# Chunkwise mLSTM: the work of a chunk split into three parts that run one and two chunks apart

## The chip, the cores and the metric

One core of a Trainium2 chip. The metric is the device time of one execution in microseconds (us), the median of several runs. TensorE is called PE, VectorE DVE, ScalarE ACT, GpSimd POOL and SyncE SP in the rows.

## What is computed

Three transformer blocks run one after the other on one sequence of 1024 tokens with 1024 features. The change is in the first block, in its mLSTM branch, which has 4 heads of 128 features and walks the sequence in 8 chunks of 128 tokens:

```python
def step(carry, inp):
    C, n, m = carry
    qb, kb, vb, ib, bb = inp
    d = bb[..., :, None] - bb[..., None, :] + ib[..., None, :]
    d = jnp.where(tri, d, -jnp.inf)
    g = bb + m[..., None]
    m_t = jnp.maximum(g, jnp.max(d, axis=-1))
    s_qk = jnp.einsum('bhtk,bhsk->bhts', qb, kb) * jnp.exp(d - m_t[..., None])
    inter = jnp.exp(g - m_t)
    num = (jnp.einsum('bhts,bhsv->bhtv', s_qk, vb)
           + inter[..., None] * jnp.einsum('bhvk,bhtk->bhtv', C, qb))
    den = jnp.sum(s_qk, axis=-1) + inter * jnp.einsum('bhk,bhtk->bht', n, qb)
    h = num / jnp.maximum(jnp.abs(den), jnp.exp(-m_t))[..., None]
    ...
    C_new = decay[..., None, None] * C + jnp.einsum('bhs,bhsv,bhsk->bhvk', wa, vb, kb)
    n_new = decay[..., None] * n + jnp.einsum('bhs,bhsk->bhk', wa, kb)
    return (C_new, n_new, m_new), h
```

Everything that depends on the running maximum m is known for all tokens before the chunks begin (rows R1, R4 and the columns COL in the kernel). Only C and n pass from chunk to chunk.

## The kernel before

The kernel is written by hand: each engine has one function for each block (`pe_block1`, `dve_block1`, `act_block1`), its instructions run in the order in which they are written, and the engines are tied by semaphores. The large products of all three blocks take their weights from one stream of 131 slots, which SP loads, POOL splits into a high and a low part, and PE uses in order. PE's products of one slot take about 22 us in block 1. Two slots of split weights and two of raw ones are held ahead of PE.

The mLSTM chunks use no streamed weights. For each of the 8 chunks the kernel before runs, in this order of dependence:

- PE, line 724: the row R4 spread over 128 partitions (bank 0), 4 products; the row R1 likewise (bank 1), line 727; then `bc_ready`. Then the keys transposed (bank 3, line 731, `kt_ready`) and the scores of keys and queries (bank 2, line 735, `sc_ready`). Each product of two fp32 operands shows as two instructions in the trace, a transpose as one.
- DVE, line 1076: the exponents into the tile EW (4 instructions, one for each head), `e_done`; ACT, line 908: the exponential over EW, `w_exp`. DVE meanwhile, lines 1079 to 1085: the scaled queries QS, the decay DEC, the weighted keys KW. Then line 1090: EW times the scores, the weights between tokens, `pt_done`.
- PE, lines 714 and 716: the numerators, from EW and the values and, from the second chunk on, QS and the state CS (banks 4 and 5), `num_ready`; line 719: the update of the state from KW (banks 6 and 7), `cu_ready`.
- DVE, lines 1095 to 1120: the new state CS, `c_done`; four small instructions for the denominator; the output h into QT (line 1112), `h_done`; its statistics (bn_stats and bn_aggr).
- ACT, line 910, sends for the sigmoid of the next chunk's output gate (OSC, two buffers) after each exponential. Line 1112 needs it.

There is one buffer each of EW, QS, KW and of every bank, and DVE's chunk begins with the exponents of this chunk, after the statistics of the last. The loop of PE is written with the second half of chunk c - 1 ahead of the first half of chunk c:

```python
for c in range(NT + 1):
    if c >= 1:
        pe.wait_ge(S("pt_done"), c)
        wait(pe, S("c_done"), c - 1)
        ...                                  # numerators and update of chunk c - 1
    if c < NT:
        ...                                  # rows, transposes, scores of chunk c
```

After the eighth chunk PE goes on with the queries of the differential attention (`q_d`, line 438), two slots that have been split long before.

Of the kernel before, what the change touches and what calls it, by code (L numbers as in the profile page):

```python
# [23 lines left out]
ACT = mybir.ActivationFunctionType  # L24
AX = mybir.AxisListType.X

P = 128
# [114 lines left out]
class Line:  # L142
# [10 lines left out]
    def wait(self, n=None):  # L153
        self.eng.wait_ge(self.sem, self.n if n is None else n)
# [16 lines left out]
def build(nc, xT, memT, stream, params, wqkv, sgu, bias2, lru_w, metaT, outT, o_scr, h_scr, blocks=(1, 2, 3)):  # L171
    TL, WH = plan(blocks)
    NSLOT = len(TL) // TILES
    with ExitStack() as ctx:
# [10 lines left out]
                 "ff_raw": ("d_sq", 32), "weight_step": ("lam_v", 2), "meta_step": ("lam_a", 1), "final_step": ("d_sd", 1), "f_sq": ("mv_done", 8),  # L185
# [19 lines left out]
        def at(name, offset, shape, dt=F32):  # L205
            return nc.alloc_sbuf_tensor_at(name, shape, dt, offset=base + offset)
# [363 lines left out]
        if 1 in blocks:  # L570
# [18 lines left out]
            EW = at("e_w", CH, [P, H1, P])  # L589
# [70 lines left out]
        def pe_block1(pe):  # L660
# [47 lines left out]
            for c in range(NT + 1):  # L708
                if c >= 1:

                    pe.wait_ge(S("pt_done"), c)
                    wait(pe, S("c_done"), c - 1)
                    for h in range(H1):
                        mm = nc.tensor.matmul(num(h), EW[:, h, :], V1[:, c - 1, h, :], start=True, stop=(c == 1))
                        if c > 1:
                            mm = nc.tensor.matmul(num(h), QS[:, h, :], CS[:, h, :], start=False, stop=True)
                    mm.then_inc(S("num_ready"), 1)
                    for h in range(H1):
                        mm = nc.tensor.matmul(cup(h), KW[:, h, :], V1[:, c - 1, h, :], start=True, stop=True)
                    mm.then_inc(S("cu_ready"), 1)  # L720
                if c < NT:
                    for h in range(H1):
                        sel = IDENT[0:4, h:h + 1].to_broadcast([4, P])
                        nc.tensor.matmul(ps[:, P * h:P * (h + 1)], sel, R4[:, P * c:P * (c + 1)], start=True, stop=True)
                    for h in range(H1):
                        sel = IDENT[0:4, h:h + 1].to_broadcast([4, P])
                        mm = nc.tensor.matmul(ps[:, BANK + P * h:BANK + P * (h + 1)], sel, R1[:, P * c:P * (c + 1)],
                                              start=True, stop=True)
                    mm.then_inc(S("bc_ready"), 1)
                    for h in range(H1):  # L730
                        mm = nc.tensor.transpose(ps[:, 3 * BANK + P * h:3 * BANK + P * (h + 1)], KT[:, h, P * c:P * (c + 1)],
                                                 IDENT)
                    mm.then_inc(S("kt_ready"), 1)
                    for h in range(H1):
                        mm = nc.tensor.matmul(ps[:, 2 * BANK + P * h:2 * BANK + P * (h + 1)], KT[:, h, P * c:P * (c + 1)],
                                              QT[:, h, P * c:P * (c + 1)], start=True, stop=True)
                    mm.then_inc(S("sc_ready"), 1)

            slot, quad = WH["q_d"]
# [102 lines left out]
        def act_block1(act):  # L844
# [60 lines left out]
            act.dma_start(OSC[:, 0, :], o_scr[0]).then_inc(S("o_back0"), 16)  # L905
            for c in range(NT):
                act.wait_ge(S("e_done"), c + 1)
                nc.scalar.activation(EW[:, :, :], EW[:, :, :], ACT.Exp).then_inc(S("w_exp"), 1)
                if c + 1 < NT:
                    act.dma_start(OSC[:, (c + 1) % 2, :], o_scr[c + 1]).then_inc(S(f"o_back{(c + 1) % 2}"), 16)  # L910
            act.wait_ge(S("mv_done"), NT)
            nc.scalar.activation(SD[:, :], MV[:, :, 1], ACT.Sqrt, bias=EPSC).then_inc(S("sd_done"), 1)

# [103 lines left out]
        def dve_block1(dve):  # L1017
# [54 lines left out]
            for c in range(NT):  # L1072
                dve.wait_ge(S("bc_ready"), c + 1)
                wait(dve, S("num_ready"), c)
                for h in range(H1):
                    ins = nc_v.scalar_tensor_tensor(EW[:, h, :], ps[:, BANK + P * h:BANK + P * (h + 1)], COL[:, c, h:h + 1],
                                                    par("mask_ts", 0, P), ALU.add, ALU.add)
                ins.then_inc(S("e_done"), 1)
                v.step(nc_v.tensor_tensor(QS[:, :, :], ps[:, 0:BANK].rearrange("p (h t) -> p h t", h=H1),
                                          QT[:, :, P * c:P * (c + 1)], ALU.mult))  # L1080
                v.step(nc_v.tensor_copy(DEC[:, :], ps[:, P - 1:BANK:P]))
                dve.wait_ge(S("kt_ready"), c + 1)
                wait(dve, S("cu_ready"), c)
                for h in range(H1):
                    v.step(nc_v.tensor_scalar(KW[:, h, :], ps[:, 3 * BANK + P * h:3 * BANK + P * (h + 1)],
                                              COL[:, c, 4 + h:5 + h], SC1, ALU.mult, ALU.mult))
                dve.wait_ge(S("w_exp"), c + 1)
                dve.wait_ge(S("sc_ready"), c + 1)
                v.wait()
                nc_v.scalar_tensor_tensor(EW[:, :, :].rearrange("p h t -> p (h t)"), ps[:, 2 * BANK:3 * BANK], SC1,  # L1090
                                          EW[:, :, :].rearrange("p h t -> p (h t)"), ALU.mult, ALU.mult).then_inc(S("pt_done"), 1)
                dve.wait_ge(S("cu_ready"), c + 1)
                for h in range(H1):
                    if c == 0:
                        ins = nc_v.tensor_copy(CS[:, h, :], cup(h))
                    else:
                        ins = nc_v.scalar_tensor_tensor(CS[:, h, :], CS[:, h, :], DEC[:, h:h + 1], cup(h), ALU.mult, ALU.add)
                    ins.then_inc(S("c_upd"), 1) if h < H1 - 1 else ins.then_inc(S("c_done"), 1)
                dn = ps[:, 4 * BANK:6 * BANK].rearrange("p (b x) -> p b x", b=2)[:, :, 0:2 * (P + 1)]\
                    .rearrange("p b (h w) -> p b h w", w=P + 1)[:, :, :, P]  # L1100
                v.step(nc_v.tensor_scalar(DN[:, :].rearrange("p (b h) -> p b h", b=2), dn, -1.0, None, ALU.mult))
                v.wait()
                v.step(nc_v.tensor_tensor(DN[:, :].rearrange("p (b h) -> p b h", b=2), dn,
                                          DN[:, :].rearrange("p (b h) -> p b h", b=2), ALU.max))
# [1492 lines left out]
```

## Time and profile before

| | |
|---|---|
| median of 3 runs | 3708.5 us (3707.46 to 3709.02) |
| the profiled execution's own time | 3712.65 us |
| its span | 3710.9 us |
| busy share: PE, DVE, ACT, POOL | 91%, 36%, 20%, 32% |
| mean granted clock of TensorE | 0.956 of full speed |

The span runs from the first to the last instruction of the profiled execution. The chunks lie between about 224 and 328 us of it. A granted clock of 1.00 is TensorE at 2.4 GHz, 0.50 at 1.2 GHz, and a value between is a stretch with some of both. A row "x8" is eight instructions in a run, with the time from the first's start to the last's end.

### The profile page before, as it was taken

To read this page: it belongs to the slowest core of one execution; us is meant where nothing else is said; L and a number is where in the kernel's file an instruction comes from. 1 tells how busy PE (TensorE), PEld (TensorE's weight loads), DVE (VectorE), ACT (ScalarE), POOL (GpSimd) and SP (SyncE) were. 2 spreads that over 40 slices of the span, in tenths; PEclk is the share of its full clock that TensorE was granted. 3 is DMA by queue.
4 is the path that set the end of the run, shared out by engine and by line. 5 is a ranking of instruction groups with operands and counts; after the bars stand their busy time and mean duration, and the time that the engine had idled before them with its cause. 6 is when DMAs were issued, how large, how long until landed. Compare 5 with 4: busy or idle time off the path is not lost.

```text
span 3710.9 us, 37478 instructions
## 1 busy us (share of the span) xinstructions
PE 3375.2 (91%) x15576; PEld 2708.9 (73%) x15576; DVE 1341.0 (36%) x1651; ACT 744.9 (20%) x1082; POOL 1194.3 (32%) x1012
## 2 busy tenths in 40 slices
PE   5967976889959999999999999997997989999997
PEld 4646854778848568877888888886984678888886
DVE  4145055033140450223342111126999662222223
ACT  2220045121021450111211000003442410001011
POOL 3201300525423013324444334433232243443341
PEclk9977998899979899999999999999999999999998
DMA  3100100101221001112111111111202011111111
GB/s 117 47 15 20 53 5 12 68 23 64 84 85 46 23 13 46 66 37 92 46 46 46 57 45 45 46 56 42 80 35 80 23 36 56 45 45 57 45 45 46
DMA packets 31693, 179.62 MB, mean 48 GB/s; under 512 B 3793, under 2 KB 4817, under 8 KB 14673
## 3 DMA queue, kind: packets, MB, share of 16 engines
q1 hardware_dynamic: 18864, 137.37, 10.5%
q10 hardware_dynamic: 12704, 40.42, 2.9%
q8 instruction: 99, 1.62, 0.2%
q14 instruction: 26, 0.20, 0.0%
HBM read 163.10 MB, written 14.68 MB: 48 GB/s over the span
## 4 chain that ended last, share of the span: by engine, by line
PE 82%; DVE 12%; ACT 3%; issue 2%; POOL 1%; DMA 0%; DVEq 0%; ACTq 0%; POOLq 0%
PE ps L438 47%; PE ps L469 16%; PE ps L495 5%; PE ps L1902 3%; DVE c_out L2353 2%; PE ps L1434 1%; PE ps L770 1%; PE ps L1450 1%; ACT p L937 1%; PE ps L678 1%; PE ps L318 1%; PE ps L326 1%; PE ps L1953 1%; DVE soft L1164 1%; DVE p L1639 1%
## 5 line engine op out<-in xcount | busy, mean ns | idle before, releaser
L535 POOL TENSOR_TENSOR whi<-raw,par 128x512 fp32r<-128x512 f32 x121 | 134.3, 1110 | 2150.8 <-PE ps L438 1703.5
L438 PE MATMUL ps<-xhi,whi 128*128 128x512 f32 x2304 | 721.4, 395 | 45.3 <-DVE xlo L379 15.2
L539 POOL TENSOR_TENSOR wlo<-raw,whi 128x512 fp32r<-128x512 f32 x484 | 716.3, 1480 | 38.5
L438 PE MATMUL ps<-xlo,whi 128*128 128x512 f32 x2304 | 716.1, 392 | 0.0
L438 PE MATMUL ps<-xhi,wlo 128*128 128x512 f32 x2304 | 714.9, 392 | 0.0
L438 PEld LDWEIGHTS ps<-xhi,whi 128*128 128x128 f32 x2304 | 434.2, 190 | 148.0 <-issue 24.3
L438 PEld LDWEIGHTS ps<-xlo,whi 128*128 128x128 f32 x2304 | 437.0, 190 | 92.3
L438 PEld LDWEIGHTS ps<-xhi,wlo 128*128 128x128 f32 x2304 | 436.1, 189 | 92.2
L537 POOL CAST whi<-raw 128x512 fp32r<-128x512 f32 x363 | 280.4, 772 | 0.0
L469 PE MATMUL ps<-hidden_hi,whi 128*128 128x512 f32 x864 | 268.6, 392 | 0.4 <-DVE hidden_lo L1314 0.4
L469 PE MATMUL ps<-hidden_lo,whi 128*128 128x512 f32 x864 | 268.8, 392 | 0.0
L469 PE MATMUL ps<-hidden_hi,wlo 128*128 128x512 f32 x864 | 267.1, 390 | 0.0
L1324 DVE TENSOR_TENSOR h<-h,ps 128x1024 f32<-128x1024 f32 x112 | 132.3, 1217 | 350.5 <-PE ps L469 350.5
L1276 ACT ACTIVATE ff_act<-ps 128x1024 f32<-128x1024 f32 x46 | 47.3, 1028 | 976.9 <-PE ps L438 976.9
L469 PEld LDWEIGHTS ps<-hidden_hi,wlo 128*128 128x128 f32 x864 | 162.2, 188 | 36.6
L469 PEld LDWEIGHTS ps<-hidden_lo,whi 128*128 128x128 f32 x864 | 162.3, 188 | 35.8
L469 PEld LDWEIGHTS ps<-hidden_hi,whi 128*128 128x128 f32 x864 | 161.3, 188 | 36.4 <-issue 1.7
L2353 DVE SCALAR_TENSOR_TENSOR c_out<-c_in,par,c_out 128x1024 f32<-128x1024 f32 x120 | 179.1, 1494 | 4.9 <-ACT c_out L2105 1.4
L547 POOL TENSOR_TENSOR wlo<-raw,whi 128x512 fp32r<-128x512 f32 x40 | 83.1, 2107 | 263.4 <-ACT whi L258 263.4
L1305 DVE TENSOR_TENSOR ff_tmp<-ff_act,ps 128x1024 f32<-128x1024 f32 x18 | 22.0, 1221 | 328.0 <-ACT ff_act L1276 328.0
L1310 DVE TENSOR_TENSOR ff_tmp<-ff_act 128x1024 f32<-128x1024 f32 x32 | 41.1, 1285 | 216.2 <-ACT ff_act L1276 216.1
L1314 DVE TENSOR_TENSOR hidden_lo<-ff_tmp,hidden_hi 128x1024 fp32r<-128x1024 f32 x54 | 86.9, 1609 | 63.8 <-ACT hidden_hi L1279 63.8
(458 smaller groups left out, 4149.8 us busy)
## 6 DMA issues: line engine op xcount, KB each, us to landing
raw<-stream SPq DMA_DIRECT2D x131, 1024.0 KB, 4.7
x_in<-xT ACTq DMA_DIRECT2D x4, 1024.0 KB, 14.6
x_again<-xT ACTq DMA_DIRECT2D x4, 1024.0 KB, 8.1
h_scr<-h ACTq DMA_DIRECT2D x1, 4096.0 KB, 12.6
h<-h_scr ACTq DMA_DIRECT2D x1, 4096.0 KB, 13.2
h_scr<-h ACTq DMA_DIRECT2D x4, 1024.0 KB, 4.7
outT<-h ACTq DMA_DIRECT2D x8, 512.0 KB, 3.0
bias<-bias ACTq DMA_DIRECT2D x1, 2560.0 KB, 18.7
```

Of the source, the lines that this page charges most:

```text
L438: mm = nc.tensor.matmul(ps[:, c0 + c:c0 + c + width], w, x(k, a, width), start=(n == 0 and m == 0), stop=(n == len(ks) - 1 and m == 2))
L469: mm = nc.tensor.matmul(ps[:, c0 + c:c0 + c + HALF], w, x(k, a, HALF), start=(k == 0 and m == 0), stop=(k == n - 1 and m == 2))
L495: mm = nc.tensor.matmul(ps[:, c:c + BANK], x(k, P * tt, P), w, start=(k == 0 and m == 0), stop=(k == KB - 1 and m == 2))
L535: nc.gpsimd.tensor_tensor(WHI[:, r, t], RAW[:, r, t], one, ALU.mult).then_inc(hi_done, 1)
L537: nc.gpsimd.tensor_copy(WHI[:, r, t], RAW[:, r, t]).then_inc(hi_done, 1)
L539: ins = nc.gpsimd.tensor_tensor(WLO[:, r, t], RAW[:, r, t], WHI[:, r, t].bitcast(F32), ALU.subtract)
L547: ins = nc.gpsimd.tensor_tensor(WLO[:, r, t], RAW[:, r, t], WHI[:, r, t].bitcast(F32), ALU.subtract)
L1276: nc.scalar.activation(FA[:, j % 2, :], half(q, 0), ACT.Silu if k == "f2" else ACT.Relu)\
L1314: nc.vector.tensor_tensor(HL[:, j, :], FT[:, j % 2, :], HH[:, j, :].bitcast(F32), ALU.subtract)\
L1324: nc.vector.tensor_tensor(stream_tile[:, b, :], stream_tile[:, b, :], half(q, b % 2), ALU.add).then_inc(free(q), 1)
L1902: mm = nc.tensor.matmul(ps[:, c0 + BANK * i:c0 + BANK * i + width], w, x(k, a, width), start=(k == 0 and m == 0), stop=(k == KB - 1 and m ...
L2353: nc.vector.scalar_tensor_tensor(CCO[:, b, :], CC[:, b, META + k:META + k + T], par("cc_conv_w_3", 4 * k + b), CCO[:, b, :], ALU.mult, ALU ...
```

## The change

The same instructions are issued, in another order. PE's work of a chunk is split into `chunk_scores` (the spread of R1 and the scores) and `chunk_rows` (the spread of R4 and the transposes), DVE's into `chunk_exponents`, `chunk_weights`, `chunk_queries` and `chunk_keys`. The scores, exponents and weights of chunk c + 2 are made in the loop's pass c, the scaled queries and weighted keys of chunk c + 1 likewise. EW has two buffers, the second over weights that are no longer needed. QS, KW and the banks stay single. The waits on DVE's own counter for QS, DEC and KW are gone, and PE waits on two new counts, `qs_done` and `kw_done`. ACT sends for the sigmoid of chunk c once h of chunk c - 2 is made, one pass earlier than before.

```diff
+            def chunk_scores(c):
+                wait(pe, S("e_done"), c)
+                for h in range(H1):
+                    ...
+                mm.then_inc(S("bc_ready"), 1)
+                wait(pe, S("pt_done"), c)
+                for h in range(H1):
+                    ...
+                mm.then_inc(S("sc_ready"), 1)
+
+            def chunk_rows(c):
+                if c > 0:
+                    pe.wait_ge(*L("qs_done", 2 * c))
+                for h in range(H1):
+                    ...
+                if c > 0:
+                    pe.wait_ge(*L("kw_done", c))
+                for h in range(H1):
+                    ...
+                mm.then_inc(S("kt_ready"), 1)
+
+            chunk_scores(0)
+            chunk_rows(0)
+            chunk_scores(1)
+            for c in range(NT):
+                pe.wait_ge(S("pt_done"), c + 1)
+                pe.wait_ge(*L("qs_done", 2 * c + 1))
+                wait(pe, S("c_done"), c)
+                wait(pe, S("h_done"), c)
+                for h in range(H1):
+                    ...
+                mm.then_inc(S("num_ready"), 1)
+                pe.wait_ge(*L("kw_done", c + 1))
+                for h in range(H1):
+                    ...
+                mm.then_inc(S("cu_ready"), 1)
+                if c + 1 < NT:
+                    chunk_rows(c + 1)
+                if c + 2 < NT:
+                    chunk_scores(c + 2)
...
-                if c + 1 < NT:
-                    act.dma_start(OSC[:, (c + 1) % 2, :], o_scr[c + 1]).then_inc(S(f"o_back{(c + 1) % 2}"), 16)
+                if c >= 1:
+                    wait(act, S("h_done"), c - 1)
+                    act.dma_start(OSC[:, c % 2, :], o_scr[c]).then_inc(S(f"o_back{c % 2}"), 16)
...
+            chunk_exponents(0)
+            chunk_queries(0)
+            chunk_keys(0)
+            chunk_weights(0)
+            chunk_exponents(1)
+            chunk_weights(1)
+            for c in range(NT):
                 dve.wait_ge(S("cu_ready"), c + 1)
+                dve.wait_ge(*L("qs_done", 2 * c + 2))
...
                 ins.then_inc(S("h_done"), 1)
+                if c + 1 < NT:
+                    chunk_queries(c + 1)
+                    chunk_keys(c + 1)
+                if c + 2 < NT:
+                    chunk_exponents(c + 2)
                 dve.wait_ge(S("h_done"), c + 1)
...
                 ins.then_inc(S("mv_done"), 1)
+                if c + 2 < NT:
+                    chunk_weights(c + 2)
```

On DVE, from the output h of one chunk (q_t) to the next update of the state. Before:

```order
L1112 SCALAR_TENSOR_TENSOR q_t<-ps,denom,o_sig 128x128 x4
L1117 BN_STATS stats<-q_t 128x6 x4
L1120 BN_AGGR mean_var<-stats 128x2 x4
L1076 SCALAR_TENSOR_TENSOR e_w<-ps,cols,par 128x128 x4
L1079 TENSOR_TENSOR q_s<-ps,q_t 128x512
L1081 COPY decay<-ps 128x4
L1085 TENSOR_SCALAR k_w<-ps,cols 128x128 x4
L1090 SCALAR_TENSOR_TENSOR e_w<-ps,e_w 128x512
L1097 SCALAR_TENSOR_TENSOR c_state<-c_state,decay,ps 128x129 x4
```

and of the change:

```order
L1149 SCALAR_TENSOR_TENSOR q_t<-ps,denom,o_sig 128x128 x4
L1109 TENSOR_TENSOR q_s<-ps,q_t 128x512
L1111 COPY decay<-ps 128x4
L1116 TENSOR_SCALAR k_w<-ps,cols 128x128 x4
L1096 SCALAR_TENSOR_TENSOR e_w_379<-ps,cols,par 128x128 x4
L1159 BN_STATS stats<-q_t 128x6 x4
L1162 BN_AGGR mean_var<-stats 128x2 x4
L1104 SCALAR_TENSOR_TENSOR e_w_379<-ps,e_w_379 128x512
L1134 SCALAR_TENSOR_TENSOR c_state<-c_state,decay,ps 128x129 x4
```

The scaled queries, the decay and the weighted keys (of the next chunk) now follow h directly; the exponents and the weights (e_w, first and last row of that tile) belong to the chunk after the next, and the statistics stand between them.

On PE, from the update of the state to the next chunk's numerators. Before:

```order
L719 MATMUL ps<-v_one,k_w 128x129 x4
L724 MATMUL ps<-row_374,par 128x128 x4
L727 MATMUL ps<-row_373,par 128x128 x4
L731 MATMUL ps<-par,k_t 128x128 x4
L735 MATMUL ps<-q_t,k_t 128x128 x4
L714 MATMUL ps<-v_one,e_w 128x129
L716 MATMUL ps<-c_state,q_s 128x129
```

and of the change:

```order
L751 MATMUL ps<-v_one,k_w 128x129 x4
L729 MATMUL ps<-row_374,par 128x128 x4
L733 MATMUL ps<-par,k_t 128x128 x4
L715 MATMUL ps<-row_373,par 128x128 x4
L720 MATMUL ps<-q_t,k_t 128x128 x4
L745 MATMUL ps<-v_one,e_w_379 128x129
L747 MATMUL ps<-c_state,q_s 128x129
```

PE's order within a chunk is nearly the same. What moved is whose they are: the spread of R1 and the scores (L715 and L720) are those of the chunk after the one whose numerators follow.

## Rows read from the trace of the kernel before

**Rows 1.** The chain of waits, 224 to 334 us: start us, us, engine, tile, line.

```profile
236.16 0.89 DVE c_state L1095 x4
...
328.33 5.77 PE ps L438 x24
```

**Rows 2.** Who waited for whom, 228 to 333 us: us in total, times, longest.

```profile
POOL whi L535 <- PE ps L438: 201.9, 1, 201.9
...
DVE c_state L1097 <- PE ps L719: 37.7, 7, 5.6
...
PE ps L714 <- DVE e_w L1090: 31.5, 8, 4.5
```

**Rows 3.** Timeline, last chunk: start us, us, engine line op [idle before <-releaser].

```profile
314.92 1.12 DVE L1097 SCALAR_TENSOR_TENSOR c_state<-c_state,decay,ps 128x129 f32<-128x129 f32 x4 [5.62 <-PE ps L719]
...
316.75 1.13 DVE L1112 SCALAR_TENSOR_TENSOR q_t<-ps,denom,o_sig 128x128 f32<-128x128 f32 x4
...
317.92 0.87 DVE L1117 BATCH_NORM_STATS2 stats<-q_t 128x6 f32<-128x128 f32 x4
...
319.12 1.09 DVE L1076 SCALAR_TENSOR_TENSOR e_w<-ps,cols,par 128x128 f32<-128x128 f32 x4
...
320.13 0.68 DVE L1079 TENSOR_TENSOR q_s<-ps,q_t 128x512 f32<-128x512 f32 x1
...
320.25 0.63 ACT L908 ACTIVATE e_w<-e_w 128x512 f32<-128x512 f32 x1 [12.82 <-DVE e_w L1076]
...
320.80 1.11 DVE L1085 TENSOR_SCALAR k_w<-ps,cols 128x128 f32<-128x128 f32 x4
...
322.05 0.69 DVE L1090 SCALAR_TENSOR_TENSOR e_w<-ps,e_w 128x512 f32<-128x512 f32 x1
...
322.80 0.80 PE L714 MATMUL ps<-v_one,e_w 128*128 128x129 f32 x2 [4.27 <-DVE e_w L1090]
...
326.40 1.93 PE L719 MATMUL ps<-v_one,k_w 128*128 128x129 f32 x8
...
328.37 1.12 DVE L1097 SCALAR_TENSOR_TENSOR c_state<-c_state,decay,ps 128x129 f32<-128x129 f32 x4 [5.62 <-PE ps L719]
```

**Rows 4.** Timeline, second chunk, TensorE after its clock rose.

```profile
247.19 1.06 PE L719 MATMUL ps<-v_one,k_w 128*128 128x129 f32 x8
...
248.18 1.15 PE L724 MATMUL ps<-row,par 4*128 4x128 f32 x8
...
250.65 1.06 PE L735 MATMUL ps<-q_t,k_t 128*128 128x128 f32 x8
```

**Rows 5.** Timeline, first chunk, TensorE.

```profile
224.72 2.04 PE L724 MATMUL ps<-row,par 4*128 4x128 f32 x8 [0.44 <-DVE cols L1068]
...
226.55 1.91 PE L727 MATMUL ps<-row,par 4*128 4x128 f32 x8
...
228.39 1.11 PE L731 MATMUL ps<-par,k_t 128*128 128x128 f32 x4
...
229.30 1.91 PE L735 MATMUL ps<-q_t,k_t 128*128 128x128 f32 x8
...
232.31 2.09 PE L714 MATMUL ps<-v_one,e_w 128*128 128x129 f32 x8 [1.10 <-DVE e_w L1090]
```

**Rows 6.** TensorE by stretches: us, busy (instructions), granted clock, DMA share, GB/s.

```profile
243.80:246.80 3.00, 3.00 (x14) 0.50 0.00 0
246.80:252.00 5.20, 4.91 (x40) 0.99 0.00 0
490.00:610.00 120.00, 88.32 (x587) 0.99 0.00 1
750.00:790.00 40.00, 30.89 (x218) 1.00 0.00 1
350.00:370.00 20.00, 13.92 (x57) 0.74 0.00 1
```

**Rows 7.** The sigmoid tile that comes back from memory, issue to landing.

```profile
DMA to landing us min/median/max: 2.4/2.6/2.7
```

More of the change, by code:

```diff
@@ L184, in build @@
                  "m_sq": ("bc_ready", 8), "m_sum": ("kt_ready", 8), "pads_set": ("sc_ready", 8), "l_cols": ("vt_ready", 8),
-                 "ff_raw": ("d_sq", 32), "weight_step": ("lam_v", 2), "meta_step": ("lam_a", 1), "final_step": ("d_sd", 1), "f_sq": ("mv_done", 8),
+                 "ff_raw": ("d_sq", 32), "qs_done": ("gate_sum", 12), "kw_done": ("qkv_kept", 12), "weight_step": ("lam_v", 2), "meta_step": ("lam_a", 1), "final_step": ("d_sd", 1), "f_sq": ("mv_done", 8),
                  "f_add": ("h_done", 8), "f_x": ("ones_set", 1), "sp_a": ("o_stored", 32), "sp_b": ("rows_a", 6),
@@ L588, in build @@
             CH = XM_AT + 8192
-            EW = at("e_w", CH, [P, H1, P])
+            EW = [at("e_w0", CH, [P, H1, P]), at("e_w1", XM_AT + 20512, [P, H1, P])]
             QS = at("q_s", CH + 2048, [P, H1, P])
@@ L707, in pe_block1 @@
             pe.wait_ge(S("cols_kept"), 1)
[L708 to L737, printed above, removed]
@@ new lines, in chunk_scores @@
+            def chunk_scores(c):
+                wait(pe, S("e_done"), c)
+                for h in range(H1):
+                    sel = IDENT[0:4, h:h + 1].to_broadcast([4, P])
+                    mm = nc.tensor.matmul(ps[:, BANK + P * h:BANK + P * (h + 1)], sel, R1[:, P * c:P * (c + 1)],
+                                          start=True, stop=True)
+                mm.then_inc(S("bc_ready"), 1)
+                wait(pe, S("pt_done"), c)
+                for h in range(H1):
+                    mm = nc.tensor.matmul(ps[:, 2 * BANK + P * h:2 * BANK + P * (h + 1)], KT[:, h, P * c:P * (c + 1)],
+                                          QT[:, h, P * c:P * (c + 1)], start=True, stop=True)
+                mm.then_inc(S("sc_ready"), 1)
@@ new lines, in chunk_rows @@
+            def chunk_rows(c):
+                if c > 0:
+                    pe.wait_ge(*L("qs_done", 2 * c))
+                for h in range(H1):
+                    sel = IDENT[0:4, h:h + 1].to_broadcast([4, P])
+                    nc.tensor.matmul(ps[:, P * h:P * (h + 1)], sel, R4[:, P * c:P * (c + 1)], start=True, stop=True)
+                if c > 0:
+                    pe.wait_ge(*L("kw_done", c))
+                for h in range(H1):
+                    mm = nc.tensor.transpose(ps[:, 3 * BANK + P * h:3 * BANK + P * (h + 1)], KT[:, h, P * c:P * (c + 1)], IDENT)
+                mm.then_inc(S("kt_ready"), 1)
@@ new lines, in pe_block1 @@
+            chunk_scores(0)
[7 more added lines that the diff above has]
+                for h in range(H1):
+                    mm = nc.tensor.matmul(num(h), EW[c % 2][:, h, :], V1[:, c, h, :], start=True, stop=(c == 0))
+                    if c > 0:
+                        mm = nc.tensor.matmul(num(h), QS[:, h, :], CS[:, h, :], start=False, stop=True)
+                mm.then_inc(S("num_ready"), 1)
+                pe.wait_ge(*L("kw_done", c + 1))
+                for h in range(H1):
+                    mm = nc.tensor.matmul(cup(h), KW[:, h, :], V1[:, c, h, :], start=True, stop=True)
+                mm.then_inc(S("cu_ready"), 1)
[3 more added lines that the diff above has]
+                    chunk_scores(c + 2)
@@ L907, in act_block1 @@
                 act.wait_ge(S("e_done"), c + 1)
-                nc.scalar.activation(EW[:, :, :], EW[:, :, :], ACT.Exp).then_inc(S("w_exp"), 1)
-                if c + 1 < NT:
-                    act.dma_start(OSC[:, (c + 1) % 2, :], o_scr[c + 1]).then_inc(S(f"o_back{(c + 1) % 2}"), 16)
+                nc.scalar.activation(EW[c % 2][:, :, :], EW[c % 2][:, :, :], ACT.Exp).then_inc(S("w_exp"), 1)
+                if c >= 1:
+                    wait(act, S("h_done"), c - 1)
+                    act.dma_start(OSC[:, c % 2, :], o_scr[c]).then_inc(S(f"o_back{c % 2}"), 16)
             act.wait_ge(S("mv_done"), NT)
@@ L1071, in dve_block1, with chunk_exponents @@
             dve.wait_ge(S("skip_done"), 4)
-            for c in range(NT):
+            def chunk_exponents(c):
                 dve.wait_ge(S("bc_ready"), c + 1)
-                wait(dve, S("num_ready"), c)
+                wait(dve, S("num_ready"), c - 1)
                 for h in range(H1):
-                    ins = nc_v.scalar_tensor_tensor(EW[:, h, :], ps[:, BANK + P * h:BANK + P * (h + 1)], COL[:, c, h:h + 1],
+                    ins = nc_v.scalar_tensor_tensor(EW[c % 2][:, h, :], ps[:, BANK + P * h:BANK + P * (h + 1)], COL[:, c, h:h + 1],
@@ L1077, in dve_block1, with chunk_weights @@
                                                     par("mask_ts", 0, P), ALU.add, ALU.add)
                 ins.then_inc(S("e_done"), 1)
-                v.step(nc_v.tensor_tensor(QS[:, :, :], ps[:, 0:BANK].rearrange("p (h t) -> p h t", h=H1),
-                                          QT[:, :, P * c:P * (c + 1)], ALU.mult))
-                v.step(nc_v.tensor_copy(DEC[:, :], ps[:, P - 1:BANK:P]))
-                dve.wait_ge(S("kt_ready"), c + 1)
+            def chunk_weights(c):
+                dve.wait_ge(S("w_exp"), c + 1)
+                dve.wait_ge(S("sc_ready"), c + 1)
+                e = EW[c % 2][:, :, :].rearrange("p h t -> p (h t)")
+                nc_v.scalar_tensor_tensor(e, ps[:, 2 * BANK:3 * BANK], SC1, e, ALU.mult, ALU.mult).then_inc(S("pt_done"), 1)
@@ L1083, in dve_block1, with chunk_queries, chunk_keys @@
+            def chunk_queries(c):
+                dve.wait_ge(S("kt_ready"), c + 1)
+                wait(dve, S("num_ready"), c)
+                nc_v.tensor_tensor(QS[:, :, :], ps[:, 0:BANK].rearrange("p (h t) -> p h t", h=H1),
+                                   QT[:, :, P * c:P * (c + 1)], ALU.mult).then_inc(*qs_step)
+                nc_v.tensor_copy(DEC[:, :], ps[:, P - 1:BANK:P]).then_inc(*qs_step)
+            def chunk_keys(c):
                 wait(dve, S("cu_ready"), c)
                 for h in range(H1):
-                    v.step(nc_v.tensor_scalar(KW[:, h, :], ps[:, 3 * BANK + P * h:3 * BANK + P * (h + 1)],
-                                              COL[:, c, 4 + h:5 + h], SC1, ALU.mult, ALU.mult))
@@ L1087, in dve_block1 @@
[L1087 to L1091, printed above, removed]
+                    ins = nc_v.tensor_scalar(KW[:, h, :], ps[:, 3 * BANK + P * h:3 * BANK + P * (h + 1)],
+                                             COL[:, c, 4 + h:5 + h], SC1, ALU.mult, ALU.mult)
@@ L1092, in dve_block1 @@
+                ins.then_inc(S("kw_done"), 1)
+            qs_step = (S("qs_done"), 1)
+            chunk_exponents(0)
[5 more added lines that the diff above has]
+            for c in range(NT):
                 dve.wait_ge(S("cu_ready"), c + 1)
+                dve.wait_ge(*L("qs_done", 2 * c + 2))
                 for h in range(H1):
```

## Prediction

> **What bounds the kernel now.** I read the chain of waits first, to see whether the chunks lie on the path that sets the end. They do: it runs from the first state update at 236.16 to the products of `q_d` at 328.33 without a piece of other work [rows 1]. The eighth update starts at 328.37 [rows 3], so the seven chunk periods take (328.37 - 236.16)/7 = 13.17 us each. The table of who waited for whom says how such a period is made up: DVE waits for PE's line 719 for 37.7 us in 7 times and PE waits for DVE's line 1090 for 31.5 us in 8 times [rows 2]. Neither engine is full. They take turns.
>
> The timeline of the last chunk gives the turns [rows 3]. DVE works from the update at 314.92 to the end of the weights at 322.05 + 0.69 = 322.74, 7.82 us. PE then makes numerators and update, and DVE starts again 328.37 - 322.80 = 5.57 us later. 7.82 + 0.06 + 5.57 = 13.45. PE's other work (rows, transposes, scores) lies beside DVE's turn already and costs nothing today.
>
> The clock is part of it. Of the 5.57 us, 16 products take 326.40 - 322.80 = 3.60, or 0.22 us each [rows 3]. In the second chunk the granted clock is 0.50 in the first 3 us and 0.99 in the next 5.2 [rows 6], and there 8 products take 248.18 - 247.19 = 0.99, or 0.12 each [rows 4]. The idle turn drops TensorE to 1.2 GHz, and the numerators, the only part on the path, pay for it. At 2.4 GHz they and the update would be 24 x 0.124 + 0.1 = 3.1 us. Rows, transposes and scores are 250.65 + 1.06 - 248.18 = 3.53 at 2.4 GHz.
>
> **The change, step by step.** *What stays between updates.* No arithmetic is added or removed. The exponents, ACT's exponential and the weights of a chunk are now made nearly two passes before their numerators. What PE still waits for behind an update is the state, the denominator, h, and the scaled queries. The DVE pieces by [rows 3], start to start: update and denominator 316.75 - 314.92 = 1.83; h 1.01 (taken from 320.13 - 319.12, four instructions with no wait behind them; with the wait for h in front of the statistics it is 1.17); queries 0.68; signal 0.06. PE starts 3.58 us after the update starts. The next update can start 3.58 + 3.1 = 6.7 us after the last if TensorE runs at 2.4 GHz, and 3.58 + 5.57 = 9.15 at 1.2 GHz.
>
> *What DVE needs in all.* It issues the same instructions, 7.82 us by rows. Two waits on its own results fall away: behind h (1.17 - 1.01 = 0.16) and between the keys and the weights (322.05 - 320.80 = 1.25 against 1.01, so 0.24). That leaves 7.42; for the four waits on semaphores that are new in a pass I add 0.1, my estimate: **7.5 us**. The Trainium skill (VectorE: DVE Perf Modes, "The DRAIN you can't avoid") says that a semaphore between two DVE operations costs nothing extra. These rows disagree, for a wait on the operation just before. By the page the period would be 7.8, and the time 2 us more.
>
> *What PE needs in all.* 3.1 + 3.5 = 6.6 us at 2.4 GHz, beside DVE's 7.5. So DVE sets the pace, PE is 88% busy, and the 3.5 us of rows and scores lie in the 3.58 us in which PE waits for the queries; at 1.2 GHz they would not. Of PE's queue: `q_d` stands behind the last update only; the scores of chunk c + 2 wait for the weights of chunk c + 1, which DVE ended before it began this pass.
>
> *ACT and the transfer.* The exponential, 0.63 us [rows 3], has the statistics on DVE as cover, 319.12 - 317.92 = 1.20 us; without them DVE would wait 0.7. ACT's new wait for h stands in front of its DMA; that h was made before the exponents that ACT has just handled, so nothing queued behind it (the next exponential) is late. The sigmoid lands 2.6 us after issue [rows 7] and is wanted more than one pass later. SP and POOL get no new wait. POOL has stood 201.9 us waiting for PE when `q_d` begins [rows 2], so the weights are split and `q_d` simply starts earlier.
>
> *The start.* More must be done before the first numerators. Before, the first update starts 236.16. Now PE makes at 1.2 GHz the spread of R1, the scores and the spread of R4 (8 instructions each, 226.55 - 224.72 = 1.83) and 4 transposes (229.30 - 228.39 = 0.91) [rows 5]: ready at 224.72 + 6.4 + 0.2 = 231.3. DVE adds queries and decay 0.67, keys 1.01, weights 0.7: 233.8. Scores of chunk 1, 1.84, then numerators and update as before (236.16 - 232.31 = 3.85 [rows 1, 5]): 239.5 if the clock stays low. It rose near 236 before; I take 239.0, so **+2.8 us**.
>
> *The sum.* Pass 0: 7.3 (its update is a copy, 0.15 shorter). Passes 1 to 5: 5 x 7.5 = 37.5. Pass 6 makes no exponents or weights, so DVE needs 5.9 and the path through PE, 6.7, decides. 239.0 + 7.3 + 37.5 + 6.7 = 290.5, and 0.5 more because pass 0 may begin at the low clock: 291.0. Before: 328.37. **Saved: 37.4 us.** Behind the loop nothing changes but the start. The profiled execution has a span of 3710.9 and its own time is 3712.65; the sum makes that 3675.3. It lies 4.15 above the median of the runs, 3708.5, and the same step off the median gives **3671 us**.
>
> *The clock.* This is the term that the trace before does not show: TensorE 88% busy with gaps near 1 us. Nearest rows: in the memory attention it is busy 30.89 of 40 us with clock 1.00, and in the differential attention 88.32 of 120 at 0.99, both with small products and short gaps [rows 6]. Against them stand the transposes from 350 us on, busy 13.92 of 20 us at 0.74. The new loop is busier than all three, so I take 1.00, and keep 1.2 GHz throughout as the other end. Part of its work are products over 4 rows only; in [rows 5] the clock stays low through them.
>
> The Trainium skill (TensorE: Matmul & The Clock Gate, "A second HAM failure mode: psum-queue depth-cycling") warns that frequent short idles between groups of matmuls make the clock go up and down. By it the answer would be rival B; the two attention rows of this case do not bear it out, the transposes do.
>
> **The rivals.** *A, the forecast:* high clock, DVE sets the pace. 3671, chance 0.75.
>
> *B, the clock swings.* It is low when the numerators start, high for the rows and scores. Period 9.15: 239.5 + 7 x 9.15 = 303.6, saved 24.8: **3684**. For it: the transposes in [rows 6]. Chance 0.15.
>
> *C, low clock all through.* PE needs 24 products 5.3 + 6.4 = 11.75 a chunk and sets the pace itself: 239.5 + 6 x 11.75 + 9.15 = 319.2, saved 9.2: **3699**. [...] Chance 0.04.
>
> *D, slower: the scores in lockstep.* There is one bank of scores, and PE's scores stand ahead of the numerators in its queue. If their wait were ended only by the last DVE instruction of the same pass, at the low clock, a period would be DVE's 7.42, scores 1.91, numerators and update 5.57, 14.9: 239.5 + 6 x 14.9 + 9.15 = 338, 9.7 later: **3718**. It is slower than before from a period of 13.3 us. Against it: the count in that wait asks for the weights of one pass earlier. Chance 0.03.
>
> *E, the gain does not arrive.* The chunks shrink, but a later stage that runs on a schedule of its own (split weights, loads) holds `q_d` or its successors: **3708**. Against it: POOL's 201.9 us. Chance 0.03.
>
> **How the numbers follow.** The prediction is A's 3671. Its own bounds: the start with the high clock throughout (1.5 less), a DVE period of 7.2 (1.8 less), 2 to 3 us of run differences: 3665. Upward B's 3684 and 2 us for a slower warm-up: 3686. That holds A and B, nearly 0.9; C, D and E are left out. A change below 0.2% (7.4 us) can't be told from none: A, B and most of C lie beyond it, faster 0.93; same 0.04 (E and the rest of C); slower 0.03.
>
> **What would show it.** In the trace after: the updates (c_state) some 7.5 us apart in passes 1 to 5, first near 239, last near 291; DVE with no idle time to speak of before them; PE's wait for the scaled queries near 1 us; numerators at 0.12 us an instruction and a granted clock near 1.00 from 245 to 290. Updates 9 us apart with numerators at 0.22 us would be B, 12 us apart with PE never idle C, PE idle ahead of the scores D, idle PE ahead of line 438 E. The sum is wrong if DVE's instructions grow longer beside a busy PE, or if the first update comes after 241.

## The result and the profile after

| | before | after |
|---|---|---|
| median of 4 runs | 3708.76 us | 3676.84 us (3669.43 to 3679.06) |
| span of the profiled execution | 3710.9 us | 3675.2 us |
| its granted clock | 0.956 | 0.959 |

The ratio is 0.991, interval 0.9892 to 0.9927: 31.9 us faster. For the runs made later, the kernel before had medians of 3712.3 to 3712.9, and each is compared with the one of its own group. All runs were in the same fast state but one execution of the kernel before in the last group (6841.41 us), which the ratios leave out.

Timeline of the kernel after, VectorE's state updates, and the first products of `q_d`:

```profile
239.94 0.89 DVE L1132 COPY c_state<-ps 128x129 f32<-128x129 f32 x4 [2.67 <-PE ps L751]
...
248.29 1.12 DVE L1134 SCALAR_TENSOR_TENSOR c_state<-c_state,decay,ps 128x129 f32<-128x129 f32 x4 [1.12 <-PE ps L751]
...
255.66 1.11 DVE L1134 SCALAR_TENSOR_TENSOR c_state<-c_state,decay,ps 128x129 f32<-128x129 f32 x4
263.04 1.12 DVE L1134 SCALAR_TENSOR_TENSOR c_state<-c_state,decay,ps 128x129 f32<-128x129 f32 x4
...
270.41 1.11 DVE L1134 SCALAR_TENSOR_TENSOR c_state<-c_state,decay,ps 128x129 f32<-128x129 f32 x4
...
278.66 1.13 DVE L1134 SCALAR_TENSOR_TENSOR c_state<-c_state,decay,ps 128x129 f32<-128x129 f32 x4 [0.79 <-PE ps L751]
...
286.78 1.12 DVE L1134 SCALAR_TENSOR_TENSOR c_state<-c_state,decay,ps 128x129 f32<-128x129 f32 x4 [0.65 <-PE ps L751]
...
294.67 0.79 PE L438 MATMUL ps<-xhi,whi 128*128 128x512 f32 x2
295.03 1.13 DVE L1134 SCALAR_TENSOR_TENSOR c_state<-c_state,decay,ps 128x129 f32<-128x129 f32 x4 [2.40 <-PE ps L751]
```

The updates, 13.45 us apart before [rows 3], are 8.35, 7.37, 7.38, 7.37, 8.25, 8.12 and 8.25 us apart. Three that begin without an idle time in brackets follow directly on the weights: there VectorE sets the pace. The long ones have 0.65 to 2.40 us of waiting for PE's line 751. The last update is 328.37 - 295.03 = 33.3 us earlier, and `q_d` starts 327.98 - 294.67 = 33.3 earlier.

Who waited for whom, 228 to 300 us, against [rows 2]:

```profile
POOL whi L535 <- PE ps L438: 168.2, 1, 168.2
...
DVE c_state L1134 <- PE ps L751: 5.0, 4, 2.4
PEld ps L745 <- issue: 4.6, 4, 2.2
PE ps L745 <- DVE decay L1111: 3.9, 4, 2.0
```

VectorE's waits for the update fell from 37.7 to 5.0 us, PE's for the numerators' inputs from 31.5 to 3.9. POOL still waits for PE, 168.2 us.

TensorE by stretches, kernel after (us, busy, granted clock, DMA share, GB/s):

```profile
228.00:232.00 4.00, 4.00 (x18) 0.50 0.00 0
236.00:240.00 4.00, 4.00 (x20) 0.50 0.25 66
248.29:270.41 22.12, 20.89 (x163) 1.00 0.11 30
270.41:295.03 24.62, 21.97 (x136) 0.79 0.10 29
```

It is busy nearly throughout and still at 1.2 GHz up to 240 us. Between 240.1 and 248.3 the clock is up, down from 243.7 to 247.0, and up again; then come 22 us at 2.4 GHz with the three short periods, then both levels in turn. The timeline within the slow part:

```profile
274.07 0.49 PE L745 MATMUL ps<-v_one,e_w 128*128 128x129 f32 x2 [0.62 <-DVE decay L1111]
...
274.36 0.63 PE L747 MATMUL ps<-c_state,q_s 128*128 128x129 f32 x2
...
274.78 0.64 PE L745 MATMUL ps<-v_one,e_w 128*128 128x129 f32 x2
...
284.52 0.43 PE L747 MATMUL ps<-c_state,q_s 128*128 128x129 f32 x2
...
284.79 0.39 PE L745 MATMUL ps<-v_one,e_w 128*128 128x129 f32 x2
```

Two products of a head take 0.64 us, 0.43 apart, while the clock is low, and 0.39, 0.22 apart, once it is high; the clock falls at 274.4, within a run of products that began at 274.07 after 0.62 us of idling. It does not stay low until the last rows: it is back at 1.00 from 278.0 to 281.0, falls once more near 281.2 and rises at 284.5. Between 274.07 and that second fall TensorE had no idle time at all, and none from 234.39 to the fall at 243.7 either:

```profile
240.50:243.50 3.00, 3.00 (x24) 1.00 0.00 0
244.00:247.00 3.00, 3.00 (x16) 0.50 0.19 31
...
278.00:281.00 3.00, 3.00 (x25) 1.00 0.08 29
281.50:284.50 3.00, 3.00 (x14) 0.50 0.00 0
```

The last low stretch, from 291.0 on, is another case: in the last pass TensorE had stood idle for 2.03 us, up to 290.44.

Behind the loop the lead wanders. The products of `out_1` (line 438 with y_hi) start at 919.2 before and 884.3 after, 34.9 us earlier, the last of line 438 at 3635.6 and 3600.0, 35.6 earlier:

```profile
L438 PE MATMUL ps<-xhi,whi x2304: 387/389/796, 46.4 to 3635.6; 128*128 128x512 f32 x192
...
L438 PE MATMUL ps<-y_hi,whi x128: 388/394/397, 919.2 to 1044.8; 128*128 128x512 f32 x128
```

```profile
L438 PE MATMUL ps<-xhi,whi x2304: 389/389/796, 46.5 to 3600.0; 128*128 128x512 f32 x192
...
L438 PE MATMUL ps<-y_hi,whi x128: 388/394/398, 884.3 to 1010.0; 128*128 128x512 f32 x128
```

Of the span's 35.7 us, 33.3 are the loop's; the other 2.4 lie within what two executions of one kernel differ by (the four runs after spread over 9.6 us).

### The profile page after: what moved, and what is told of

It reads as the page before. It is cut to its first block, busy times and chain, and to the rows that moved or that the text cites. A ratio compares the mean times of both kernels' runs of the same rounds, so it can differ in the third digit from the quotient of the medians.

```text
span 3675.2 us, 37493 instructions
## 1 busy us (share of the span) xinstructions
PE 3368.2 (92%) x15576; PEld 2703.0 (74%) x15576; DVE 1339.0 (36%) x1651; ACT 745.2 (20%) x1082; POOL 1194.6 (33%) x1012
## 3 DMA queue, kind: packets, MB, share of 16 engines
q1 hardware_dynamic: 18864, 137.37, 10.6%
## 4 chain that ended last, share of the span: by engine, by line
PE 82%; DVE 12%; ACT 3%; issue 2%; POOL 1%; DMA 0%; DVEq 0%; ACTq 0%; POOLq 0%
PE ps L438 48%; PE ps L469 16%; PE ps L495 5%; PE ps L1946 3%; DVE c_out L2397 2%; PE ps L1478 1%; PE ps L788 1%; PE ps L1494 1%; ACT p L956 1%; PE ps L678 1%; PE ps L318 1%; PE ps L326 1%; PE ps L1997 1%; DVE soft L1208 1%; DVE p L1683 1%
## 5 line engine op out<-in xcount | busy, mean ns | idle before, releaser
L537 POOL CAST whi<-raw 128x512 fp32r<-128x512 f32 x363 | 281.0, 774 | 0.0
## 6 DMA issues: line engine op xcount, KB each, us to landing
x_in<-xT ACTq DMA_DIRECT2D x4, 1024.0 KB, 14.6
```

Of the source, the lines that this page charges most:

```text
L537: nc.gpsimd.tensor_copy(WHI[:, r, t], RAW[:, r, t]).then_inc(hi_done, 1)
```

## The experiments

The theory: the two-chunk distance and the early queries took everything but state, h and queries off the path, so that VectorE's sum sets the pace; and what is missing to the forecast in the loop is TensorE's clock, which the products over 4 rows fail to hold up. The rivals: fixed causes in the order; the short gaps; a pace set by PE.

### The change once more

No edit.

> The change itself once more, on another occasion. Every theory expects update periods of 7.4 us where TensorE has its high clock, since DVE is never idle there. Theory A (the low stretches of the clock fall anywhere in the loop): the periods that took 8.1 to 8.3 us are other ones or another number of them, and the total lies within 3 to 5 us of 3677. Rival (a fixed cause, such as the load of ACT's table or the last chunk's order): the same three periods are long again.

Measured: 3679.50 us (ratio 0.9911, 0.9895 to 0.9928), 32.9 us under the kernel before. Updates 8.16, 7.39, 7.36, 8.25, 8.17, 7.37 and 8.25 us apart.

```profile
247.06:261.81 14.75, 14.14 (x111) 1.00 0.09 24
261.81:293.85 32.04, 28.65 (x188) 0.84 0.11 32
```

The fourth period is now long and the sixth short, so the order of the program does not fix where these two low stretches fall. The first, the fifth and the last period were long both times; for them two executions do not rule out a fixed cause.

### Spreads over all rows

```diff
-            R1 = at("row_1", XM_AT, [4, T])
-            R4 = at("row_4", XM_AT + 4096, [4, T])
+            R1W = at("row_1", XM_AT, [P, T])
+            R4W = at("row_4", XM_AT + 4096, [P, T])
+            R1, R4 = R1W[0:4, :], R4W[0:4, :]
...
-                    sel = IDENT[0:4, h:h + 1].to_broadcast([4, P])
+                    sel = IDENT[:, h:h + 1].to_broadcast([P, P])
```

Both tiles are set to zero once, where VectorE waits for the gates; the products read R1W and R4W.

> The change, with the spread of R1 and R4 made by products over all 128 rows (the other 124 are zero) instead of 4 rows; as many instructions. Theory (products over 4 rows do not hold TensorE's clock up): granted clock 1.00 from the first update to the last, all periods 7.4 us, the first update some 1 us earlier than 239.9, the last 4 to 6 us earlier than 295.0, total 3671 to 3673. Rival (the idle 0.6 us in each pass lowers the clock): low stretches as before, last update near 295, total 3677.

Measured: 3672.66 us (0.9893, 0.9876 to 0.9909), 39.8 under before, 6.8 under the change of the same group (four executions of each, 3671.1 to 3674.1 and 3678.3 to 3680.7, though the intervals of the two ratios overlap). Updates 7.14, five times 7.37 or 7.38, then 8.25 us apart.

```profile
226.00:230.00 4.00, 2.79 (x23) 0.94 0.00 0
240.51:277.37 36.86, 30.16 (x262) 1.00 0.12 37
```

The first spread starts 2.0 us earlier here than in the kernel after (222.81 against 224.81), so 226 to 230 us here corresponds to 228 to 232 there. The clock is 0.94 from 226 to 230 us and 1.00 over the next six periods. In the kernel after it was 0.50 from 228 to 232 with 4.00 of 4 us busy. The 2.79 us busy here don't mean that idling helps: the clock rose near 226.2, with TensorE busy since the first spread, and the idle time (1.59 us from 228.80) came after that. In the kernel after 9.09 us without a break left it at 0.50:

```profile
224.81:233.90 9.09, 9.09 (x36) 0.50 0.12 31
```

Once up, the clock stayed at a busy share of 82% here (30.16 of 36.86 us, with an idle time of 1.33 us in each pass), while the kernel after lost it at 94% (20.89 of 22.12, idle times of 0.61 us). So what fills the busy time matters. That it is all that matters is not shown: see the late statistics below. The last period is as long as in the change, 8.25 us, with full rows too. There TensorE is idle for 3.12 us, and the clock falls at 281.1, just after the numerators have begun. From the first spread to the last update it takes 285.62 - 222.81 = 62.8 us, against 295.03 - 224.81 = 70.2 for the change. 4.6 of these 7.4 us lie in front of the first update (233.37 - 222.81 = 10.6 against 239.94 - 224.81 = 15.1). I had expected 1 us there; the clock now rises before the first numerators.

### The same rows in the kernel before

The same edit on the kernel before.

> The kernel before with the spread of R1 and R4 over all 128 rows. Theory (in the old loop the clock falls because of PE's 4.4 us idle turn, whatever the rows): periods stay at 13.0 to 13.5 us, numerators start at the low clock, total 3705 to 3712; only the first chunk may gain 1 to 2 us. Rival (the 4-row products are what lowered the clock there too): periods near 11 us and a total near 3695.

Measured: 3712.58 us (0.9998, 0.9988 to 1.0008): no change. The periods are 12.98 to 13.45 us but for the first. With an idle turn of 4.4 us in each chunk the rows do not change the periods. At the start they do: from the first spread to the first update it takes 235.16 - 225.67 = 9.5 us, against 236.16 - 224.72 = 11.4 before, the 1 to 2 us that I had expected there. The total, with its interval of about 4 us to either side, does not show them.

### A filler in the kernel before

```diff
+                    wait(pe, S("c_done"), c - 1)
+                    if c >= 2:
+                        for _ in range(16):
+                            nc.tensor.matmul(ps[:, 7 * BANK + 384:8 * BANK], IDENT, KT[:, 0, 0:P], start=True, stop=True)
                     pe.wait_ge(S("pt_done"), c)
-                    wait(pe, S("c_done"), c - 1)
```

> The kernel before, with 16 products into unread columns of bank 7 in PE's idle turn ahead of the numerators. Theory (half of the old path through PE was the low clock): the granted clock is near 1.00, numerators and update take 3.1 instead of 5.57 us, the period falls from 13.2 to about 11, total 3691 to 3694. Rival (the clock plays no part in those 5.57 us, or the filler itself delays the numerators): period 13 us or more, total 3708 or above.

Measured: 3697.83 us (0.996, 0.9946 to 0.9975), 14.6 under before. The updates are 10.86 or 10.87 us apart, but for the first period (10.63).

```profile
247.24:312.43 65.19, 59.85 (x505) 1.00 0.08 21
```

```profile
261.36 3.74 PE L714 MATMUL ps<-k_t,par 128*128 128x128 f32 x32
...
265.98 0.49 PE L717 MATMUL ps<-v_one,e_w 128*128 128x129 f32 x2 [0.89 <-DVE e_w L1093]
...
266.31 0.39 PE L719 MATMUL ps<-c_state,q_s 128*128 128x129 f32 x2
...
267.87 1.06 PE L722 MATMUL ps<-v_one,k_w 128*128 128x129 f32 x8
...
268.97 0.87 DVE L1100 SCALAR_TENSOR_TENSOR c_state<-c_state,decay,ps 128x129 f32<-128x129 f32 x3 [3.04 <-PE ps L722]
```

The first fence is the stretch, the second the timeline: filler, numerators, update of the state on PE, then VectorE. From 265.98 to 268.97 are 2.99 us, where the kernel before took 5.57. 13.45 - 10.87 = 2.58 us a chunk came from the clock alone, with the old order. The total is 3.8 us above the upper end of what I wrote down; the kernel before of this group is 3.7 above its earlier median.

### One chunk ahead instead of two

```diff
...
                     chunk_keys(c + 1)
-                if c + 2 < NT:
-                    chunk_exponents(c + 2)
+                    chunk_exponents(c + 1)
+                    chunk_weights(c + 1)
...
-                if c + 2 < NT:
-                    chunk_scores(c + 2)
+                if c + 1 < NT:
+                    chunk_scores(c + 1)
...
```

The scores, exponents and weights of chunk 1 ahead of the loop and the old place of the weights, behind the statistics, go too.

> The change with the scores, exponents and weights one chunk ahead of the state instead of two, made behind the scaled queries and keys; statistics last, no second product in flight. Theory (the distance of two chunks is what takes exponents, exponential and weights off the path): the path from update to numerators is then 1.83 + 1.01 + 0.67 + 1.01 + 1.01 + 0.8 (ACT) + 0.7 = 7.0 us, the period 10.2 at the high clock and up to 12.6 at the low one, the last update near 315 to 325, total 3700 to 3705. Rival (the new waits between queries and PE are what matters, one chunk ahead is as good): periods of 7.4 to 8.3 us, total 3680.

Measured: 3708.19 us (0.999, 0.998 to 1.0), 4.1 under before: nearly all of the gain is gone. Periods 11.49 to 13.01 us, last update 325.43, at or just beyond the far end of what I expected, the total 3 us beyond it. Who waited for whom, 240 to 325 us:

```profile
DVE c_state L1131 <- PE ps L750: 23.8, 6, 4.4
...
PE ps L744 <- DVE e_w L1103: 18.8, 7, 3.3
DVE e_w L1103 <- ACT e_w L925: 4.2, 6, 0.7
```

The engines take turns again, and VectorE waits for the exponential (4.2 us in 6 times) that had cover in the change. The clock is low through most of the numerators again (0.50 from 255 to 264 us, for one), so the loss is that of the turns and of the clock together; the run does not part the two.

### Queries and keys last

```diff
                 if c + 2 < NT:
                     chunk_weights(c + 2)
+                if c + 1 < NT:
+                    chunk_queries(c + 1)
+                    chunk_keys(c + 1)
```

with their old place, behind h, empty.

> The change with scaled queries and weighted keys made at the end of DVE's pass, behind exponents, statistics and weights, as late as before. Theory (early queries are the other half): from update to numerators 1.83 + 1.01 + 1.01 + 1.2 + 0.6 + 0.68 + 0.1 = 6.4 us, period 9.5 us at the high clock, 11.9 at the low one; PE idles some 3 us a pass, so the clock will be low for part of the numerators; total 3690 to 3702. Rival (DVE's sum sets the pace whatever its order): periods 7.4 us, total 3679.

Measured: 3703.96 us (0.9978, 0.9969 to 0.9988), 8.4 under before. Periods 10.05 to 12.00 us, last update 317.65; the total is 2 us beyond what I expected. So VectorE's sum does not set the pace by itself. Undone singly, either part costs most of the gain: the one leaves 4, the other 8 of 33 us. The pace of 7.4 us needs both.

### Statistics behind the loop

```diff
                 if c + 1 < NT:
                     chunk_queries(c + 1)
-                    chunk_keys(c + 1)
                 if c + 2 < NT:
                     chunk_exponents(c + 2)
+                if c + 1 < NT:
+                    chunk_keys(c + 1)
...
+            dve.wait_ge(S("h_done"), NT)
+            for c in range(NT):
+                wait(dve, S("mv_done"), c)
+                ...
```

The weights of chunk c + 2 follow the keys directly.

> The change, with the statistics of all eight outputs taken behind the loop instead of in it, and the keys made after the exponents. DVE then needs 7.4 - 1.2 = 6.2 us a pass, so if DVE sets the pace now, the path through PE (3.58 + 3.1 = 6.7 us) takes over: periods 6.7 us at the high clock, the last update near 290 to 292, some 10 us of statistics beside the products of q_d, total 3 to 4 us less than the change. Rival (PE sets the pace already): periods stay at 7.4 us and the total at 3677; or the statistics come too late for the transposes behind q_d and the gain is lost there.

Measured: 3675.74 us (0.9901, 0.9884 to 0.9917), 3.8 under the change of its group. Five periods of 6.95 us; timeline:

```profile
261.13 1.16 PE L751 MATMUL ps<-v_one,k_w 128*128 128x129 f32 x8
...
262.33 1.12 DVE L1134 SCALAR_TENSOR_TENSOR c_state<-c_state,decay,ps 128x129 f32<-128x129 f32 x4 [0.66 <-PE ps L751]
...
268.08 1.16 PE L751 MATMUL ps<-v_one,k_w 128*128 128x129 f32 x8
...
269.28 0.87 DVE L1134 SCALAR_TENSOR_TENSOR c_state<-c_state,decay,ps 128x129 f32<-128x129 f32 x3 [0.65 <-PE ps L751]
```

VectorE waits 0.65 us for PE in each, so the pace has gone over to PE, as expected where VectorE set it before. The period is 6.95, not 6.7: the keys, now behind the exponents, come 0.25 us late for line 751. The statistics end at 304.7 us, 13.6 after the last update at 291.13, and PE is busy with `q_d` until 313.

By this run alone PE could be bound by its own work, since it has hardly any idle time left:

```profile
248.43:283.18 34.75, 34.42 (x261) 1.00 0.14 39
```

The next run, `late_full`, decides it: with full rows PE is busy only 31.49 of 34.75 us, and the period is 6.95 all the same. It is the path from the update through queries, keys and PE back to the update.

The row shows something else that goes against the theory in its plain form. The 16 instructions over 4 rows are still in each pass here, and the clock was 1.00 for these 34.75 us. With an idle time of under 0.1 us a pass the clock stayed up with 4 rows; with 1.33 us it stayed up with 128 rows; with 4 rows and 0.61 us it did not last. The two falls in the kernel after that came with no idle time before them show that idling is not what triggers each fall. How rows and idle time act together these runs leave open.

### Both, and a filler for the last pass

`late_full` has the full rows and the late statistics together; `full_rows2` and `late_full2` are the full rows alone and `late_full` once more. `late_full_tail` adds, ahead of the last numerators and behind the wait for the state, which moves up for it:

```diff
+                if c == NT - 1:
+                    for _ in range(8):
+                        nc.tensor.matmul(ps[:, 7 * BANK + 384:8 * BANK], IDENT, KT[:, 0, 0:P], start=True, stop=True)
```

> Both measures on top of the change: full rows for the spreads and the statistics behind the loop. If the two add up: granted clock 1.00, periods of 6.8 to 6.95 us from the first chunk, last update near 282, total 3668 to 3670, which is 4 us below the run with full rows alone. Rival (without the statistics PE, 6.6 us of work in 6.9, is the bound in another way, or the last pass costs more since its idle time lowers the clock): no more than 1 us better than full rows alone.

> Full rows for the spreads, once more, beside the next two. Periods of 7.4 us with the clock at 1.00, and a long last period; total 39 to 40 us under the kernel before.

> Full rows and late statistics, once more. By the periods (6.95 against 7.37 in six passes) the loop is 2.5 us shorter than with full rows alone; total 41 to 43 us under the kernel before. Rival: the order makes up for it behind the loop and the two totals are equal.

> As the last, with 8 products into unread columns of bank 7 in the last pass, where PE has no scores left to make and stood idle some 3 us before the last numerators. Theory (that idle time lowers the clock for the last numerators): the last period falls from 8.1 to about 6.7 us, and the first products of q_d run at the high clock; total 1 to 2 us under the last. Rival: the last period stays at 8.1 us.

| | median, us | ratio to before (interval) | first spread to last update, us | last period, us |
|---|---|---|---|---|
| late_full | 3672.04 | 0.9885 (0.9868 to 0.9901) | 287.91 - 227.21 = 60.7 | 8.14 |
| full_rows2 | 3674.00 | 0.9893 (0.9875 to 0.9911) | 290.37 - 227.03 = 63.3 | 8.25 |
| late_full2 | 3668.69 | 0.9885 (0.9867 to 0.9902) | 281.39 - 222.79 = 58.6 | 6.62 |
| late_full_tail | 3668.39 | 0.9876 (0.9858 to 0.9894) | 284.19 - 225.75 = 58.4 | 6.62 |

In the loop the two measures add up: 6.95 us a period and clock 1.00. In the totals the intervals overlap, and I can't say that late statistics gain anything on full rows alone. `late_full` ended 2 us above what I had expected, `full_rows2` is 38.9 and `late_full2` 44.2 us under the kernel before of its group, the one just short of and the other beyond what I wrote down. Of the 63.3 - 58.6 = 4.7 us between these two in the loop, where I had expected 2.5, 1.6 are the last period. On the filler of the last pass the runs decide nothing: the last period is 6.62 us with it, but also in `late_full2`, which has none and where TensorE was idle for 2.37 us as in `late_full` (8.14 us). The total is 0.3 us under `late_full2`, where 1 to 2 were expected. All four lie below both kernels in the median. `late_full_tail` is 3712.92 - 3668.39 = 44.5 us under the kernel before of its group, where the change was 31.9 and 32.9 under those of its own.

## Why the prediction was right, and where it was off

**Which wait bounds, and what goes.** Right. The turns of the two engines ended, and most of PE's idle time with them. The two runs that undo one part each show that both are needed.

**VectorE's 7.5 us.** Right in kind, slightly high: 7.37. The step by rows (7.42, two waits saved) is the better. In the kernel after the keys with what follows them take 274.98 - 273.95 = 1.03 us where they took 1.25 with a wait behind them. By the rule of the Trainium skill (VectorE: DVE Perf Modes, "The DRAIN you can't avoid"), that a semaphore costs nothing extra, the period would have been 7.8, and the trace disagrees.

**The path through PE, 3.58 + 3.1.** Right: 2.99 us for numerators and update at the high clock in the run with the filler, and with late statistics and full rows the path is what bounds, at 6.95 with its late keys, and 6.62 in the last pass of `late_full2`.

**The start, +2.8 us.** It was 239.94 - 236.16 = 3.8. The clock did not rise near 236 but near 240. The products over 4 rows that stand in front are the cause: over 128 rows the clock rose before the first numerators, and from the first spread to the first update it took 10.6 us instead of 15.1.

**The clock, taken as 1.00.** This is the term that was mis-sized. It was 1.00 throughout in three periods of seven. By rows, the last update came 4.0 us after the 291.0 of the sum: start 0.9; pass 0, 0.5 (8.35 against 7.8); passes 1 to 3, 0.4 less; passes 4 and 5, 1.4 more (16.37 against 15.0); pass 6, 1.6 (8.25 against 6.7). That is 33.3 us saved in the loop where 37.4 were forecast. The rival that the clock swings was half true, with a smaller price: a slow period was 8.1 to 8.3 and not 9.15, since the clock is low for only a part of the numerators and update, and VectorE's own 7.37 hides part of the rest. My evidence, the busy share of the attention stretches, was the wrong measure: the loop was busier than they and still lost the clock. The sentence on the products over 4 rows named a part of the cause, and I gave it no price; with full rows the loop kept 1.00 over six periods and came out at 62.8 us instead of 70.2. It does not explain the 1.6 us of pass 6: that period is 8.25 us with full rows as well, where the clock fell behind an idle time of 3.12 us (2.03 in the change). In `late_full2` it did not fall in that pass, and the period was 6.62. The Trainium skill (TensorE: Matmul & The Clock Gate, "A second HAM failure mode: psum-queue depth-cycling") tells of a kernel in which frequent short idles between groups of products made the clock go up and down. Here they were not enough by themselves, since with full rows they were longer (1.33 us a pass against 0.61) and the clock stayed up; that the late statistics, which take them away, kept the clock up with 4 rows agrees with it.

**Behind the loop.** Right: `q_d` started 33.3 us earlier and nothing held it. ACT's new wait and the earlier transfer cost nothing; VectorE never waited for the sigmoid.

**The number.** 3671 was forecast and 3676.84 measured, inside the stated range. Of the 5.8 us, 4.0 are the loop. Another 4.0 come from the step from the profiled execution to the median, taken as 4.15 from the kernel before, which was 3676.99 - 3676.84 = 0.15 this time. Against them stand the 2.4 us that the profiled execution gained outside the loop. To rounding this is all; the last two terms are run differences, and that they partly cancel is luck.

## What to carry over

When two engines take turns, look for work of either that does not depend on the carried state, and take all of it off the path: undoing one of two parts cost 24.5 to 28.8 of 32.9 us here. Then recompute who sets the pace from each engine's sum, because the next measure (here the statistics) must go there. The old loop paid twice for TensorE's idle turns, by the turn and by the low clock after it: filling the turns with useless products gained 14.6 us with the order of the work unchanged. What TensorE's clock does in a new loop did not follow from the busy share of other stages; the price of the low clock belongs in the sum until a trace shows otherwise.

## What the runs showed that I had not expected

- In the first chunks, products over 4 rows among the others left TensorE's clock low although the engine was busy: granted clock 0.50 through 9.09 us without a break. With the same number of products over 128 rows, with zeros, it rose before the first numerators and then stayed at 1.00 at a busy share of 82%. From the first spread to the first update it took 14.9 to 15.1 us in the four runs that start like the change with 4 rows, and 10.4 to 11.1 in the five with 128; with the same edit the kernel before was quicker there by 1.9 us as well. All of them rest on one edit, and 4 and 128 are the only numbers of rows tried.
- The 4 rows do not always cost the clock: with the late statistics it was 1.00 for 34.75 us with them.
- The wider products are also shorter in the stream: eight take 234.06 - 233.17 = 0.89 us over 128 rows and 263.25 - 262.16 = 1.09 over 4, both at the high clock.

```profile
233.17 1.05 PE L730 MATMUL ps<-row,par 128*128 128x128 f32 x8
...
234.06 0.60 PE L734 MATMUL ps<-par,k_t 128*128 128x128 f32 x4
```

```profile
262.16 1.15 PE L729 MATMUL ps<-row,par 4*128 4x128 f32 x8
...
263.25 0.66 PE L733 MATMUL ps<-par,k_t 128*128 128x128 f32 x4
```
